# Each piece of weight as three matmuls of 256 columns in one half of a PSUM bank

## The reference

```
h = RMSNorm(x) * (1 + scale(c)) + shift(c)          # scale, shift, gate: silu(c) @ w_ada + b_ada
z = h @ W_in                                        # 2048 -> 14336 columns, in eight groups
y_conv = gb * causal_conv3(gc * u) * silu(g)        # 2048 channels
y_ret  = GroupNorm(retention(rope(q), rope(k), v)) * silu(gr)   # 8 heads, dk 128, dv 256
x = x + gate(c) * RMSNorm(concat(y_conv, y_ret) @ W_out)        # 4096 -> 2048
```

## Time and profile before

| | |
|---|---|
| time, median of 3 runs (lowest, highest) | 1891.98 us (1888.89, 1894.93) |
| profiled execution, first to last instruction (span) | 1889.6 us |
| mean granted TensorE clock | 0.973 |
| PE busy | 1787.6 us (95%), 9855 matmuls |
| PEld busy | 1510.1 us (80%), 9855 loads |
| DVE busy | 1229.4 us (65%) |
| ACT busy | 811.7 us (43%) |
| POOL busy | 194.1 us (10%) |
| HBM read | 407 MB, 217 GB/s over the span |

### The profile page before, as it was taken

One profiled execution on the slowest core, in us unless ns is written; L12 is line 12 of the kernel. 1 busy time (PEld: TensorE's weight loads), 2 busy tenths in 40 slices (PEclk: granted clock), 3 DMA queues, 4 the chain that ended last, 5 costly groups with the idle time before them and its releaser, 6 DMA issues.

```text
span 1889.6 us, 28049 instructions
## 1 busy us (share of the span) xinstructions
PE 1787.6 (95%) x9855; PEld 1510.1 (80%) x9855; DVE 1229.4 (65%) x1486; ACT 811.7 (43%) x1054; POOL 194.1 (10%) x129
## 2 busy tenths in 40 slices
PE   6779998999899899999998999899989989999997
PEld 3358887888788788888887788788878878888886
DVE  1367887786778777864547566657666765666554
ACT  2233443444344434454444344443544443445443
POOL 5010101010110101000001010101011010100001
PEclk9799999999999999999999999999999999999998
DMA  9977785678667677855552656555655646565551
GB/s 351 346 275 267 265 273 204 240 253 268 222 215 282 201 267 253 286 179 178 181 176 89 208 198 223 178 192 191 222 178 196 239 154 216 206 215 186 197 182 45
DMA packets 223250, 410.89 MB, mean 217 GB/s; under 512 B 7168, under 2 KB 40496, under 8 KB 222896
## 3 DMA queue, kind: packets, MB, share of 16 engines
q1 hardware_dynamic: 223008, 409.46, 62.5%
q10 hardware_dynamic: 144, 0.13, 0.1%
HBM read 407.46 MB, written 2.10 MB: 217 GB/s over the span
## 4 chain that ended last, share of the span: by engine, by line
PE 80%; DVE 11%; issue 3%; DMA 2%; ACT 1%; SPq 1%; POOL 0%; DVEq 0%; ACTq 0%; POOLq 0%
PE Z L999 43%; PE Z L997 23%; DVE acc L643 6%; DVE w_lo L622 3%; PE Z L1016 3%; PE Z L1017 3%; PE Z L1018 3%; PE Z L996 2%; DMA stage<-in_w_ada 1%; DMA yr<-in_x 1%; PE SC L1134 1%; DVE bufC L815 1%; PE SC L1051 0%; ACT lo_sb L439 0%; DMA stage<-in_w_in 0%
## 5 line engine op out<-in xcount | busy, mean ns | idle before, releaser
L999 PE MATMUL Z<-H,w_hi 128*128 128x512 f32 x3392 | 1201.6, 397 | 0.0
L997 PE MATMUL Z<-H,w_lo 128*128 128x256 f32 x3584 | 974.8, 281 | 6.2 <-DVE w_lo L622 4.7
L622 DVE TENSOR_TENSOR w_lo<-stage,w_hi 128x1024 fp32r<-128x1024 f32 x576 | 711.7, 1259 | 402.6 <-ACT w_hi L433 370.6
L433 ACT CAST w_hi<-stage 128x1024 fp32r<-128x1024 f32 x576 | 592.0, 1050 | 664.8 <-PE Z L999 470.9
L999 PEld LDWEIGHTS Z<-H,w_hi 128*128 128x128 f32 x3392 | 638.1, 188 | 144.1
L997 PEld LDWEIGHTS Z<-H,w_lo 128*128 128x128 f32 x3584 | 677.4, 189 | 33.9 <-DVE w_lo L622 12.2
L643 DVE SCALAR_TENSOR_TENSOR acc<-stage,c_silu,acc 128x512 f32<-128x512 f32 x240 | 244.4, 1018 | 7.4 <-DVE w_lo L622 2.1
L999 PE MATMUL Z<-Y,w_hi 128*128 128x512 f32 x480 | 169.5, 396 | 0.0
L439 ACT COPY lo_sb<-Z 128x256 f32<-128x256 f32 x224 | 82.0, 372 | 182.3 <-PE Z L999 147.6
L1016 PE MATMUL Z<-w_hi,H 128*128 128x512 f32 x256 | 109.2, 427 | 38.7 <-DVE w_lo L622 38.2
L997 PE MATMUL Z<-Y,w_lo 128*128 128x256 f32 x512 | 137.6, 279 | 0.0
(11 more groups left out here) (147 smaller groups left out, 922.0 us busy)
## 6 DMA issues: line engine op xcount, KB each, us to landing
stage<-in_w_in SPq DMA_DIRECT2D x192, 1024.0 KB, 5.3
stage<-in_w_ada SPq DMA_DIRECT2D x96, 1024.0 KB, 7.2
stage<-in_w_out SPq DMA_DIRECT2D x64, 1024.0 KB, 5.1
stage<-in_w_in SPq DMA_DIRECT2D x64, 512.0 KB, 5.9
dec<-decay SPq DMA_DIRECT2D x9, 256.0 KB, 5.1
yr<-in_x SPq DMA_DIRECT2D x2, 1024.0 KB, 11.4
out<-stage SPq DMA_DIRECT2D x8, 256.0 KB, 2.5
bufC<-in_positions ACTq DMA_DIRECT2D x1, 128.0 KB, 5.5
```

The costliest lines, as they stand in the source:

```text
L433: nc.scalar.copy(w_hi[:, 2 * parity + h, :, :], stage[:, slot, 2 * h:2 * h + 2, :]).then_inc(s_hi, 1)
L622: V.tensor_tensor(w_lo[:, 2 * parity + h, :, :], stage[:, slot, 2 * h:2 * h + 2, :], w_hi[:, 2 * parity + h, :, :].bitcast(F32), ALU.subtr ...
L997: ins = T.matmul(Z[t][:, 0:S], wl, act[:, 0:S], start=False, stop=False)
L999: ins = T.matmul(Z[t][:, :], wh, act, start=False, stop=stop)
```

## The change

The three products of a piece become three matmuls of 256 columns, all into the left half of the bank. ACT's copy takes the left half in place of the right one, and DVE's step becomes a copy from `lo_sb` in place of an addition of the other half. The V block, all waits, all semaphore counts, the weight buffers and the DMAs are as they were.

```diff
             def z_low(pe, t, zlo, z):
                 act.wait_ge(s_pe, pe)
                 act.wait_ge(s_z, z)
-                nc.scalar.copy(lo_sb[:, t % 2, :], Z[t][:, S:2 * S]).then_inc(s_zlo, 1)
+                nc.scalar.copy(lo_sb[:, t % 2, :], Z[t][:, 0:S]).then_inc(s_zlo, 1)
...
             def z_out_of(t, zlo, dst):
                 dve.wait_ge(s_zlo, zlo)
-                V.tensor_tensor(dst, Z[t][:, 0:S], lo_sb[:, t % 2, :], ALU.add).then_inc(s_z, 1)
+                V.tensor_copy(dst, lo_sb[:, t % 2, :]).then_inc(s_z, 1)
...
                     start = kc == 0 and a == 0
                     stop = kc == nk - 1 and a == CK - 1
-                    if start:
-                        T.matmul(Z[t][:, :], wh, act, start=True, stop=False)
-                    ins = T.matmul(Z[t][:, 0:S], wl, act[:, 0:S], start=False, stop=False)
-                    if not start:
-                        ins = T.matmul(Z[t][:, :], wh, act, start=False, stop=stop)
+                    T.matmul(Z[t][:, 0:S], wh, act[:, 0:S], start=start, stop=False)
+                    T.matmul(Z[t][:, 0:S], wl, act[:, 0:S], start=False, stop=False)
+                    ins = T.matmul(Z[t][:, 0:S], wh, act[:, S:2 * S], start=False, stop=stop)
```

## The result

The changed kernel takes 1928.0 us (1927.3 to 1929.4, four runs), 1.0188 times the kernel before [1.0173, 1.0203]. It is 1.9% slower, where I had forecast 0.6% faster, and the time lies above my range.

A forecast was written before the change was run, and what follows sets the result against it. The prediction took PE's steps in `chunk` to bound the kernel. Its terms, −10 − 2 + 1 = −11 us on a span of 1889.6, gave 1878.6, with the runs' median 2.4 above the span 1881 us; range 1860 to 1912.

The forecast's parts named there:

- What bounds the kernel: PE holds 80% of the chain that ended last; two lines of `chunk` hold 65.5% of the span.
- The eight stalls: PE's waits for `w_lo` in the V block, once a turn: 38.2 us, up to 4.8 us each, expected to stay.
- the 353.3 and 346.7 levels: Two steady times of a piece on PE in the kernel before, 353.3 ns at 290 us and 346.7 ns at 1700 us.
- PE, the price of a step: In `chunk`, 116.0 ns a 256-wide step, 348.0 ns a piece instead of 350.6: −10 us, bounds −57 and +36.
- The double steps: Two 256-wide matmuls in a row at a block's start: 231.7 ns for two, taken as the price of the new steps.
- The rule that speaks against it: Added time could belong to each matmul, not its columns; the skill's N/2.4 + 2.5 ns gives +10 us over 3872 pieces.
- Rival C: Fixed charge per matmul on PE: a third adds 15.3 ns × 3872 = +59 us, 1950 us; chance 0.07.
- Theory 1: From the experiments, not the prediction: each fp32r matmul with its load costs 13.3 ns over its columns, whatever their number.
- Rival B: PE's pieces at the upper level, +10 us, or on the 120 ns step, +36 us: 1901 to 1927 us; chance 0.20.
- DVE: 224 additions of 423 ns become copies of 300 ns: −28 us of busy time, −2 us on the path, bounds −11 and 0.
- Instruction supply: PE's stream grows by 8192 instructions, fetches from 61 to some 90: +1 us, bounds 0 and +33.
- rival D: PE short of instructions: a longer loop body costs at each loop edge, up to +33 us, 1885 to 1914 us; chance 0.07.

The follow-up runs named there:

- the first program: A program of its own, fp32r chains of 48 matmuls with loads, nothing else running: 512 columns 226.7 ns a step, 256 columns 119.8 ns.
- the chains: Programs of their own with 512- and 256-column matmuls in turns or grouped by two, nothing else running: on repeating, 352.9 ns a pair in turns, 349.2 by two.
- the grouped kernel: The kernel before with the four matmuls of two neighbouring pieces as narrow, narrow, wide, wide: 1880.8 us, 0.9941 of the kernel before.
- the emptying alone: The kernel before with the changed kernel's two emptying lines (ACT's copy from the left half, DVE's copy) and its own matmuls: 1888.5 us, 0.9986.
- The written-out kernel: The changed kernel with PE's turn loops written out: 1919.9 us, 1.0141 of the kernel before.

## Why the prediction was wrong

**What bounds the kernel** was right: PE's steps in `chunk`, where the net loss is. The eight stalls, the 353.3 and 346.7 levels and the counts stand as read.

**PE, the price of a step** is what failed. I took 116.0 ns for a 256-wide step; it is 120.0 (119.9 on the mean of all). The term −10 us is measured at +38.2: 359.8 − 350.5 = 9.3 ns for each of 4096 pieces (the first pieces of a tile included, which I had at 0). The double steps of the earlier trace rows were "the same operation and not a neighbour of it", I wrote. They were a neighbour: narrow steps inside a stream with wide ones. There the profile shows 116 for a narrow step and 234 for a wide one, and a wide step in a uniform stream takes 226 to 227 (and 226.7 in the first program). Where the 234 are 7 longer, the 116 are 4 shorter than in a uniform stream, so that the two can't be priced apart. The right use of the earlier trace rows was a uniform chain with 13 ns over its columns, which gives 106.7 + 13 = 120. The last sentence of the prediction had named this weak point: a third matmul and load that cost where the double steps did not, "because there a wide matmul is never far".

**The rule that speaks against it.** I dismissed a fixed charge because 21 and 9.5 ns over the columns are in the ratio of the columns. That test took the split of the pair between its two starts at its word. For uniform chains with full loads the charge is close to fixed. Rival C had the mechanism nearest to this and mis-sized it: half of the 30.6 ns in the mixed stream, 15.3 in place of 13.3, and so 1950 us. In the two levels of the earlier trace rows the quicker one has the size of two charges (320 + 26.7 = 346.7); the slower one holds 6.6 ns more, which the change does away with. That these come from wide and narrow in turns is borne out by the chains (353 in turns, 349 by two) and by the grouped kernel, but the same order also ran at 346.7. Theory 1 alone, from the quicker level, would give 13.3 a piece; the mean is 9.3 because the mixed stream wasn't at its best.

**Rival B** named 120 ns and 1927 us, for a reason that isn't the one found: it saw 120 as one of three recurring values. The upper bound of the term, +36 us, was right within 2. My range ended at 1912 and cut it off, which was the second mistake: the bounds of this one term were −57 and +36, and I gave the whole of B, 1901 to 1927 us, a chance of 0.20.

**DVE.** 300 ns forecast, 293 measured; −2 us forecast, −3 measured by the emptying alone (between −5 and −1).

**Instruction supply** (rival D). I took +1 and it is some +8, at two of the seven loop edges, against no gap in the earlier trace rows. It is a second step that failed: that neither PE loop showed a gap before said nothing of a longer body. The written-out kernel shows what it costs; in the changed kernel's total it is hidden, since as much waiting went elsewhere. 118 fetches in place of the 90 that I scaled up from 61: by the fetches' start times the kernel before has none between 1190 and 1685 us, in the later turns of layer 1, where the changed one has 32. So in layer 1 its loop body is fetched anew in every turn, and that alone costs no pause there.

**What was to show it:** the distance of 360 named C and the upper B, and is there; the pause without a releaser named D, and is there.

**Open:** why a wide matmul beside narrow ones costs 7 ns more than in a uniform stream and the narrow ones 4 less; what picks the level in the kernel (with nothing else running the order does); how the load enters, since with 256 streamed columns 64 weight columns cost less than both 32 and 128, and whether the charge is the matmul's or its load's; why nothing is charged at the half clock; and why the loop edges of layer 0 pause and those of layer 1 don't.

## What to carry to other kernels

Price a step from a uniform chain of the same format, or from the sum over a whole period of the pattern, and never from one kind of step in a mixed stream. In fp32r at the full clock count matmuls as well as columns, some 13 ns for each with its load: two narrow ones with the same weights want to be one wide one. In a mixed stream the saving is smaller: 9.3 ns a piece here. Where a row gives a recurring value at the edge of a bound, keep it in the range.

## What the runs showed of the hardware

- With full loads at the full clock an fp32r matmul in a chain of its own kind takes its columns plus 11.7 to 16.0 ns (13.1 to 13.4 at 256, 320, 384 and 512), down to a floor of 111 to 112 ns; a bf16 one with 256 columns plus 2.5 ns. Loading the same weights again is no cheaper than loading others (119.8 ns).
- At half the clock a 256-wide fp32r matmul takes its columns alone: 213 ns.
- The order of the same matmuls moves a pair by 4 to 5 ns with nothing else running (some 353 in turns, 348 to 349 by two). In this kernel the grouped order gave 2.0 ns a piece, 8 us, and the time fell by 11 us.
- A longer body of PE's loop brought two pauses, of 2.90 and 2.96 us, at its back edges in layer 0, each followed by half the clock for 3 to 6 us; written out, the same instructions ran without one.
